# Differential attention: who splits the q, k and v weights, when a finished head is turned, and where the modulation is computed

## The chip, the core and the metric

The kernel runs on one core of a Trainium2 chip. The metric is the device time of one execution in microseconds.

## The reference

`reference` is a stack of two models at 256 tokens and 1024 features, in fp32. The first one has four blocks. Each block has a mixer (0 and 3 Fourier, 1 differential attention, 2 MLA) and a squared-ReLU MLP with 4096 hidden features. Its two inputs, the latent tokens (256) and the context tokens (256), are modulated by 6 vectors of a block, which come from a condition: one condition for the latent tokens, one for the context. The second model (two blocks with a state space mixer and window attention) is not touched by the change.

```
for i in range(DEPTH):
    sh_a, sc_a, g_a, sh_m, sc_m, g_m = split(silu(c) @ mod_w[i] + mod_b[i], 6)     # the same with c_ctx for the context
    h = rms_norm(x, norm_mix_g[i]) * (1 + sc_a) + sh_a
    x = x + g_a * mixer(h_lat, h_ctx)
    h = rms_norm(x, norm_mlp_g[i]) * (1 + sc_m) + sh_m
    x = x + g_m * (square(relu(h @ mlp_w1[i])) @ mlp_w2[i])
# differential attention, 8 heads with two maps of 64 features and a value of 128 each
p = softmax(q1 @ k1.T * scale) - lam * softmax(q2 @ k2.T * scale)      # latent queries: 512 keys, context queries: 256
y = concat(rms_norm(p @ v, subln_g) * (1 - lam_init)) @ w_o
```

Only the latent tokens leave the first model, and block 3's Fourier mixer does not read the context. So of block 2's modulation the context needs shift and scale ahead of the mixer alone (8 of 24 chunks), and of block 3's nothing.

## The kernel before

**Weights.** Every fp32 weight is used as the sum of a high and a low part, with three matmuls in the fast fp32 form (`mm3`, lines 424 to 426) for one product. Weights come in chunks of 1 MB (1024 rows by 256 columns, one `dense` chunk), in the order of `chunks`. SP loads them into raw buffers. `act_split` (L371) copies a chunk to its high part `wh`; `dve_split` (L387) and `pool_split` (L399) subtract to get the low part `wl`, VectorE the first 5/8 of the 2048 columns, GpSimd the rest (`share`, `cut`). There are three slots of `wh`/`wl`. Each engine's instructions are written out in program order, and a split for chunk c is done for c + 2 when the engine comes to chunk c: its slot is that of c - 1, so ScalarE waits until TensorE has used c - 1.

**Raw buffers.** `homes` gives each chunk its raw buffer and `sp_load` loads in the order `self.order`, waiting for the buffer's last user. As long as modulation chunks are still to come, dense chunks alternate between buffers 0 and 1, and modulation chunks use buffer 2 and, every second one in the MLPs, a fourth buffer (`extra`), which lies over other small tiles. Where no modulation chunk is to come, dense chunks take the oldest of three buffers.

**Modulation.** It is computed in two ways. A `mod` chunk is a chunk of `mod_w`: `pe_mod` (L468) multiplies it by the conditions with eight fp32 matmuls of 32 columns by 256 (two passes each), ScalarE copies a pair's rows (`act_mod`, L505), `pe_turn` (L482) turns them with four transposes, and `dve_add` (L523, L525) sums them and adds the bias. A `dmod` chunk is a chunk of the transposed `mod_w`: `pe_condition` (L490) spreads a condition over a PSUM bank pair, and `dve_dmod` (L541 for the context's condition, L546 for the latent one) multiplies and sums in one instruction, two halves of 1024 for a chunk and condition. Block 2's first 16 chunks are `mod` chunks inside the differential attention, one behind each of the twelve q, k and v chunks and four in its tail; its last 8 and the 24 of block 3 are `dmod` chunks in the second MLP, for the latent condition alone.

**Differential attention.** Twelve dense chunks q0 k0 v0 ... q3 k3 v3 (two heads each) and four of w_o. TensorE does a chunk in four parts ("half" 0 to 3). Between the parts lie the attention's steps, `pe_diff_step(s)`, two for three parts, by `beat`: steps 0 to 26 fall into the chunks, 27 to 36 follow one another in the tail, with six or more of the k-blocks of `pe_wo` between them. Unit s is a quarter (128 queries) of head s // 4. In step s TensorE turns the probabilities of unit s - 2 (L1301), computes the scores of s (L1310) and the values of s - 3 (L1321); VectorE takes the maxima (L1469, L1471), ScalarE the exponentials (L1383) and the copy of the turned probabilities (L1392), VectorE joins the two maps (L1489 to L1494). The turn of s waits for the copy of the turn before, which stands behind ScalarE's exponentials of the step, which wait for the maxima. A head's sum is scaled and squared on ScalarE in step 4h + 6 (L1403, L1407), its root is taken on VectorE in step 4h + 7 (L1503 to L1516), and in step 4h + 8 it is turned (`dx`, L1329), copied high (L1413) and low (L1479). The rotary part of q and k (`dve_rope`: L1152, the cosine product L1153, L1156) stands ahead of a step's maxima. Rope, `dx` and the modulation's turns share bank 6.

Where a norm's root is awaited, TensorE is kept at work by fillers (`pe_busy`, L628) or by the condition groups.

Of the kernel before, what the change touches and what calls it, by code (L numbers as in the profile page):

```python
# [111 lines left out]
def chunks(a):  # L112
# [18 lines left out]
    for L in range(4):  # L131
# [5 lines left out]
        elif L == 1:  # L137
            for j in range(4):
                for i, p in enumerate("qkv"):
                    w(("qkv", p, j), a["diff_w_qkv"][0], 0, 8, 1024 * i + 256 * j, 256)  # L140
                    mods(2, 3 * j + i, 3 * j + i + 1)
            mods(2, 12, 16)
# [11 lines left out]
        for n in range(32):  # L154
# [46 lines left out]
class K:  # L201
    def __init__(self, nc, a, out, known):
# [12 lines left out]
        late = [c for c in extra if c > self.ix["mod", 2, 0]]  # L215
        self.extra_first = {extra[0]: (0, 9), late[0]: (2, 7)}
        self.junked = None
        self.dmod_last = [max(c for c, p in enumerate(self.P) if p[0][0] == "dmod" and (p[0][1] < 2) == first) for first in (True, False)]
        self.extra_last = extra[len(extra) - len(late) - 1], late[-1]
# [79 lines left out]
    def homes(self):  # L299
# [78 lines left out]
    def dve_split(self, c, ahead=SLOTS):  # L378
        nc, at, up, DVE = self.nc, self.T.at, self.T.up, self.DVE
        while self.n_dve < self.split_upto(c, ahead):  # L380
# [112 lines left out]
    def act_mod(self, c):  # L493
# [9 lines left out]
        if L == 2 and h < 2:  # L503
            ACT.wait_ge(*at("used", self.extra_last[0]))
# [22 lines left out]
    def dve_dmod(self, c, m):  # L527
# [3 lines left out]
        st = "mlp0" if L < 2 else "mlp1"  # L531
# [3 lines left out]
        if L < 2:  # L535
# [2474 lines left out]
```

## Time and profile before

| | |
|---|---|
| median of 3 runs (lowest, highest) | 3154.44 us (3153.7, 3158.66) |
| the profiled execution's own time | 3153.51 us |
| its span | 3152.2 us |
| mean granted TensorE clock | 0.991 |
| PE, DVE, ACT, POOL busy | 96%, 57%, 47%, 36% of the span |
| first MLP | 165 to 525.3 us |
| differential attention | 525.3 to 831.5 us |
| second MLP | 831.5 to 1189.5 us |
| MLA | 1189.5 to 1340 us |
| third MLP | 1340 to 1531 us |

Times are microseconds from the span's start, unless marked ns. PE is TensorE, PEld its weight load, DVE VectorE, ACT ScalarE, POOL GpSimd, SPq the queue that issues the loads. A row of the timeline has the start, the length, engine, line, operation, what it writes and reads, how many, and in brackets how long its engine was idle before it and what released it. A matmul's length reaches over the start of the next one; the distance of two starts is what one costs.

### The profile page before, as it was taken

To read this page: it belongs to the slowest core of one execution; us is meant where nothing else is said; L and a number is where in the kernel's file an instruction comes from. 1 tells how busy PE (TensorE), PEld (TensorE's weight loads), DVE (VectorE), ACT (ScalarE), POOL (GpSimd) and SP (SyncE) were. 2 spreads that over 40 slices of the span, in tenths; PEclk is the share of its full clock that TensorE was granted. 3 is DMA by queue.
4 is the path that set the end of the run, shared out by engine and by line. 5 is a ranking of instruction groups with operands and counts; after the bars stand their busy time and mean duration, and the time that the engine had idled before them with its cause. 6 is when DMAs were issued, how large, how long until landed. Compare 5 with 4: busy or idle time off the path is not lost.

```text
span 3152.2 us, 49948 instructions
## 1 busy us (share of the span) xinstructions
PE 3025.6 (96%) x20560; PEld 2620.6 (83%) x20560; DVE 1783.2 (57%) x3141; ACT 1486.6 (47%) x2511; POOL 1132.0 (36%) x440
## 2 busy tenths in 40 slices
PE   5999999999999998999999999999999999999999
PEld 3878887776788886699899977878999978779999
DVE  3367775565656446665565555664465466654554
ACT  3453333344443324655465446654355356554553
POOL 0223223110332232245355432444545423434554
PEclk8999999999999999999999999999999999999999
DMA  9345552432456542155345432434555433334554
GB/s 294 121 161 191 196 197 90 142 102 86 139 196 242 200 140 74 52 168 182 112 154 187 143 118 79 119 101 128 169 164 172 149 103 108 97 114 162 159 187 139
DMA packets 423217, 459.92 MB, mean 146 GB/s; under 512 B 9040, under 2 KB 406224, under 8 KB 422992
## 3 DMA queue, kind: packets, MB, share of 16 engines
q1 hardware_dynamic: 419680, 453.32, 44.6%
q8 instruction: 164, 2.69, 0.4%
q10 hardware_dynamic: 3312, 3.42, 0.3%
q14 instruction: 61, 0.50, 0.0%
HBM read 455.66 MB, written 1.05 MB: 145 GB/s over the span
## 4 chain that ended last, share of the span: by engine, by line
PE 83%; DVE 10%; ACT 5%; issue 1%; DMA 1%; ACTq 0%; POOL 0%; DVEq 0%
PE bank L424 23%; PE bank L426 22%; PE bank L425 22%; ACT wh L371 2%; DVE wl L387 1%; PE banks L424 1%; PE banks L425 1%; PE banks L426 1%; PE banks L468 1%; PE bank L628 1%; DVE tmp L730 1%; DVE bc L2488 1%; PE banks L2451 1%; PE bank L1310 1%; DVE xl L738 1%
## 5 line engine op out<-in xcount | busy, mean ns | idle before, releaser
L399 POOL TENSOR_TENSOR wl<-raw,wh 128x768 fp32r<-128x768 f32 (+2 forms) x336 | 1013.9, 3018 | 1845.2 <-ACT wh L371 1835.2
L371 ACT ACTIVATE wh<-raw 128x2048 fp32r<-128x2048 f32 (+1 forms) x336 | 635.9, 1893 | 456.6 <-PE bank L426 423.2
L387 DVE TENSOR_TENSOR wl<-raw,wh 128x1280 fp32r<-128x1280 f32 (+2 forms) x336 | 486.6, 1448 | 524.2 <-ACT wh L371 515.4
L424 PE MATMUL bank<-nh,wh 128*128 128x272 f32 (+1 forms) x1712 | 506.8, 296 | 3.4 <-DVE nl L2036 2.8
L426 PE MATMUL bank<-nh,wl 128*128 128x272 f32 (+1 forms) x1712 | 494.2, 289 | 0.0
L425 PE MATMUL bank<-nl,wh 128*128 128x272 f32 (+1 forms) x1712 | 492.7, 288 | 0.0
L424 PE MATMUL bank<-xh,wh 128*128 128x512 f32 (+2 forms) x1282 | 441.4, 344 | 5.1 <-DVE xl L738 3.7
L426 PE MATMUL bank<-xh,wl 128*128 128x512 f32 (+2 forms) x1282 | 433.8, 338 | 0.0
L425 PE MATMUL bank<-xl,wh 128*128 128x512 f32 (+2 forms) x1282 | 433.7, 338 | 0.0
L424 PE MATMUL bank<-hh,wh 128*128 128x512 f32 (+1 forms) x1024 | 344.1, 336 | 0.0
L425 PE MATMUL bank<-hl,wh 128*128 128x512 f32 (+1 forms) x1024 | 344.1, 336 | 0.0
L426 PE MATMUL bank<-hh,wl 128*128 128x512 f32 (+1 forms) x1024 | 344.1, 336 | 0.0
L424 PEld LDWEIGHTS bank<-nh,wh 128*128 128x128 f32 x1712 | 326.7, 191 | 19.6 <-issue 17.7
L425 PEld LDWEIGHTS bank<-nl,wh 128*128 128x128 f32 x1712 | 326.6, 191 | 0.4
L426 PEld LDWEIGHTS bank<-nh,wl 128*128 128x128 f32 x1712 | 326.3, 191 | 0.0
L424 PEld LDWEIGHTS bank<-xh,wh 128*128 128x128 f32 (+1 forms) x1282 | 242.4, 189 | 46.2 <-issue 10.5
L426 PEld LDWEIGHTS bank<-xh,wl 128*128 128x128 f32 (+1 forms) x1282 | 242.4, 189 | 27.2
L425 PEld LDWEIGHTS bank<-xl,wh 128*128 128x128 f32 (+1 forms) x1282 | 242.6, 189 | 25.0
L424 PEld LDWEIGHTS bank<-hh,wh 128*128 128x128 f32 x1024 | 194.4, 190 | 20.0
L425 PEld LDWEIGHTS bank<-hl,wh 128*128 128x128 f32 x1024 | 194.4, 190 | 19.9
L426 PEld LDWEIGHTS bank<-hh,wl 128*128 128x128 f32 x1024 | 194.4, 190 | 19.9
L839 DVE TENSOR_TENSOR hl<-tmp,hh 128x512 fp32r<-128x512 f32 (+1 forms) x128 | 123.4, 968 | 116.5 <-ACT hh L820 116.5
(452 smaller groups left out, 5544.5 us busy)
## 6 DMA issues: line engine op xcount, KB each, us to landing
raw<-in_mlp_w SPq DMA_DIRECT2D x128, 1024.0 KB, 5.4
raw<-in_w_in SPq DMA_DIRECT2D x60, 1024.0 KB, 5.2
raw<-in_w_mlp_up SPq DMA_DIRECT2D x32, 1024.0 KB, 5.4
raw<-in_w_mlp_down SPq DMA_DIRECT2D x32, 1024.0 KB, 5.1
raw<-in_mod_wT SPq DMA_DIRECT2D x30, 1024.0 KB, 5.4
extra<-in_mod_wT SPq DMA_DIRECT2D x30, 1024.0 KB, 5.6
raw<-in_mod_w SPq DMA_DIRECT2D x23, 1024.0 KB, 5.2
raw<-in_w_in SPq DMA_DIRECT2D x34, 512.0 KB, 4.5
```

Of the source, the lines that this page charges most:

```text
L371: nc.scalar.activation(self.wtile(self.wh, c1), self.rawtile(c1), AF.Copy).then_inc(*up("act_wh", ("wh", c1)))
L387: nc.vector.tensor_tensor(l, r, h.bitcast(F32), ALU.subtract).then_inc(*up("dve_wl", ("wl_dve", c1)))
L399: nc.gpsimd.tensor_tensor(l, r, h.bitcast(F32), ALU.subtract).then_inc(*up("pool_wl", ("wl_pool", c1)))
L424: nc.tensor.matmul(o, ah, bh, start=first, stop=False)
L425: nc.tensor.matmul(o, ah, bl, start=False, stop=False)
L426: return nc.tensor.matmul(o, al, bh, start=False, stop=last)
L468: ins = nc.tensor.matmul(b[q:q + 32, 256 * (i % 2):256 * (i % 2) + 256], self.cst[:, k, :], w[:, k, :], start=(k < 4), stop=(k >= 4))
L628: nc.tensor.matmul(self.bank[bank][:, 0:256], self.ident[:], self.cols[:, 0:256], start=True, stop=True)
L730: nc.vector.scalar_tensor_tensor(out=self.tmp[k % 4][:, cs], in0=self.X[:, k, cs], scalar=A[:, k, s:s + 1], in1=self.spread_root(name)[:, cs],
L738: nc.vector.scalar_tensor_tensor(out=self.xl[:, k, cs], in0=self.tmp[k % 4][:, cs], scalar=self.modv[:, L, 8 * sh + k, s:s + 1], in1=self. ...
L839: nc.vector.tensor_tensor(L[i // 8 % 2][:, i % 8, T], self.ring(st)[i % 4][:, T], H[i // 8 % 2].bitcast(F32)[:, i % 8, T], ALU.subtract).t ...
L1310: nc.tensor.matmul(b[:, 0:ks.stop - ks.start], self.dtile("q", h)[rows, 128 * q:128 * q + 128], self.dtile("k", h)[rows, ks], start=True, ...
```

## The change

It has three parts. **Split.** The chunks of q, k and v get `share` 8: VectorE makes the whole low part, GpSimd none. In all of them but the first, `dve_split` moves from the head of the chunk to the place behind part 1's step, so behind its maxima. **Turns.** `finished` gives the step in which a head is turned and copied: 4h + 9 for heads 0 to 4, 4h + 8 as before for 5 to 7. In the tail `pe_wo(4, 0, 7)` stands in step 35 and `pe_wo(5, 0, 7)` behind step 36. **Modulation.** Block 2's 16 `mod` chunks and all their turns, copies and sums leave the attention. They become `dmod` chunks in the second MLP, the first eight for both conditions, which needs the bank pair 6 and 7 and two more condition groups there. The second MLP then has 36 `dmod` chunks (two behind each dense chunk 8 to 11 and 16 to 19, one behind the others up to 27); the last 12 of block 3 go to the third MLP, one behind every second dense chunk up to 22, all in raw buffer 2, with their own condition groups (`mlp2`) in place of fillers. Dense chunks alternate between buffers 0 and 1 inside the three stretches with modulation chunks only; in the attention they now have three buffers. Cut parts of the diff are the same removals on ScalarE, the same shift of `finished`, and the bookkeeping of the extra buffer and of the last user of the condition banks.

```diff
@@ -137,9 +137,7 @@
                 for i, p in enumerate("qkv"):
-                    w(("qkv", p, j), a["diff_w_qkv"][0], 0, 8, 1024 * i + 256 * j, 256)
-                    mods(2, 3 * j + i, 3 * j + i + 1)
-            mods(2, 12, 16)
+                    w(("qkv", p, j), a["diff_w_qkv"][0], 0, 8, 1024 * i + 256 * j, 256, 8)
@@ -161,12 +159,12 @@
                 dmods(1, n - 4, n - 3)
-            elif L == 1 and n < 8:
-                dmods(2, 16 + n, 17 + n)
-            elif L == 1 and n < 12:
-                dmods(3, 2 * n - 16, 2 * n - 14)
             elif L == 1 and n < 28:
-                dmods(3, n - 4, n - 3)
+                i = n + max(0, min(n, 12) - 8) + max(0, min(n, 20) - 16)
+                for i in range(i, i + (2 if n // 4 in (2, 4) else 1)):
+                    dmods(2 + i // 24, i % 24, i % 24 + 1)
+            elif L == 2 and n < 24 and n % 2 == 0:
+                dmods(3, 12 + n // 2, 13 + n // 2)
@@ -305,14 +303,16 @@
         dmods = [c for c in mods if self.P[c][0][0] == "dmod"]
+        stage = lambda c: 0 if c not in dmods else int(self.dmod_stage(c)[-1])
+        spans = [([c for c in mods if stage(c) == i][0], [c for c in mods if stage(c) == i][-1]) for i in range(3)]
...
                 d = self.nth[c]
-                t = d % 2 if self.dense[max(d - 4, 0)] < mods[-1] else min(range(RAWS), key=lambda i: last[i])
+                t = d % 2 if any(lo < c and self.dense[max(d - 4, 0)] < hi for lo, hi in spans) else min(range(RAWS), key=lambda i: last[i])
...
                 t = m % EARLY if m < 2 * EARLY else (2, 5, 6, 7)[m - 2 * EARLY] if m < 20 else 2
-                if c in dmods and dmods.index(c) % 2:
+                if c in dmods and stage(c) < 2 and dmods.index(c) % 2:
@@ -321,10 +321,19 @@
-            while late and d > 3 and (late[0] < self.dense[d - 3] or c == self.ix["wo", 2] and late[0] < self.ix["mod", 2, 14]):
+            while late and d > 3 and late[0] < self.dense[d - 3]:
...
+    def dmod_stage(self, c):
+        _, L, i = self.P[c][0]
+        return "mlp0" if L < 2 else "mlp1" if L == 2 or i < 12 else "mlp2"
+    def dmod_conditions(self, c):
+        _, L, i = self.P[c][0]
+        return 2 if L < 2 or L == 2 and i < 8 else 1
@@ -384,7 +393,7 @@
             r, h, l = self.rawtile(c1)[:, 0:n], self.wtile(self.wh, c1)[:, 0:n], self.wtile(self.wl, c1)[:, 0:n]
-            nc.vector.tensor_tensor(l, r, h.bitcast(F32), ALU.subtract).then_inc(*up("dve_wl", ("wl_dve", c1)))
+            nc.vector.tensor_tensor(l, r, h.bitcast(F32), ALU.subtract).then_inc(*up("dve_wl", ("wl_dve", c1), *([("wl_pool", c1)] if n == self.P[c1][2] * self.P[c1][3] else [])))
@@ -392,6 +401,9 @@
             n = self.cut(c1)
+            if n == self.P[c1][2] * self.P[c1][3]:
+                self.n_pool += 1
+                continue
@@ -528,11 +538,11 @@
         _, L, i = self.P[c][0]
-        st = "mlp0" if L < 2 else "mlp1"
+        st, S = self.dmod_stage(c), self.dmod_conditions(c)
...
         DVE.wait_ge(*at("raw", c))
-        if L < 2:
+        if S == 2:
@@ -599,12 +609,13 @@
     def pe_root(self, name, T):
-        if name in ("mlp0", "mlp1"):
+        if name in ("mlp0", "mlp1", "mlp2"):
...
             self.pe_condition(name, 0, 1)
-            if name == "mlp0":
+            if name == "mlp2":
+                self.pe_busy(1)
+            else:
                 self.pe_condition(name, 1, 0)
-            self.pe_busy(1 if name == "mlp1" else 0)
@@ -1182,6 +1193,13 @@
+    def finished(self, s):
+        for h in range(8):
+            if s == (9 if h < 5 else 8) + 4 * h:
+                return h
+        return None
@@ -1219,8 +1237,6 @@
                             roping = None
-                        if st == 1:
-                            self.pe_turn()
@@ -1247,27 +1263,17 @@
                             roping = None
-                        if half == 1:
-                            self.pe_turn()
...
                             roping = w, 2 * j + m
-                self.pe_mod(c + 1, (7,), (6,))
...
             self.pe_diff_step(s)
-            if s == 28:
-                self.pe_turn()
-            if s in (27, 29, 34):
-                self.pe_mod(self.ix["mod", 2, 12 + (27, 29, 34).index(s)], (7,) if s < 30 else (3,), (6,))
-            if s == 31:
-                self.pe_turn()
-            if 29 <= s < 33 or s == 35:
-                self.pe_wo(min(s - 29, 4), 0, 6)
+            if 29 <= s < 33:
+                self.pe_wo(s - 29, 0, 6)
+            elif s >= 35:
+                self.pe_wo(s - 31, 0, 7)
         for g in range(8):
-            self.pe_wo(g, 6 if g < 5 else 0, 8)
-            self.pe_turn()
-            if g == 1:
-                self.pe_mod(self.ix["mod", 2, 15], (3,), (6,))
+            self.pe_wo(g, 6 if g < 4 else 7 if g < 6 else 0, 8)
@@ -1350,11 +1356,8 @@
                     self.act_diff_step(self.beat(w, j, half))
-                self.act_mod(c + 1)
...
             self.act_diff_step(s)
-            if s == 29:
-                self.act_mod(self.ix["mod", 2, 13])
@@ -1429,28 +1430,19 @@
                             roping = None
+                        self.dve_diff_step(self.beat(w, j, half))
                         if half == 1:
-                            self.dve_add()
-                        self.dve_diff_step(self.beat(w, j, half))
+                            self.dve_split(c)
...
                             roping = w, 2 * j + half // 2
-                self.dve_mod(c + 1)
...
             self.dve_diff_step(s)
-            if s == 28:
-                self.dve_add()
-            if s == 29:
-                self.dve_mod(self.ix["mod", 2, 13])
             if s == 31:
-                self.dve_add()
...
                 self.dve_resid(("wo", 2 * j + m), 1, 2, 2 * j + m, BOTH, "mlp1")
-                self.dve_add()
-            if j == 0:
-                self.dve_mod(self.ix["mod", 2, 15])
@@ -1472,8 +1464,8 @@
             self.dve_diff_root(h)
-        h, b = divmod(s - 8, 4)
-        if b == 0 and 0 <= h < 8:
+        h = self.finished(s)
+        if h is not None:
```

## Rows read from the trace of the kernel before

**Rows 1.** The page: busy time of each engine; a DMA issue's KB and landing.
```profile
PE 3025.6 (96%) x20560; PEld 2620.6 (83%) x20560; DVE 1783.2 (57%) x3141; ACT 1486.6 (47%) x2511; POOL 1132.0 (36%) x440
...
raw<-in_mlp_w SPq DMA_DIRECT2D x128, 1024.0 KB, 5.4
```

**Rows 2.** Windows: attention, second MLP, third MLP; busy us of each engine.
```profile
525.30:831.50 306.20, 288.73 (x1782) 219.69 (x1781) 182.10 (x473) 130.15 (x288) 48.62 (x22) 0.99 0.33 108
...
831.50:1189.50 358.00, 356.10 (x1596) 292.60 (x1595) 190.64 (x297) 130.19 (x152) 105.95 (x38) 1.00 0.54 189
...
1340.00:1545.00 205.00, 200.97 (x1650) 196.60 (x1648) 119.13 (x145) 108.86 (x153) 108.71 (x41) 0.99 0.54 174
```

**Rows 3.** Timeline of TensorE, steps 26 to 29: start, length, idle before it.
```profile
754.31 0.65 PE L1301 MATMUL banks<-ident,de 128*128 128x128 f32 x4
...
758.18 0.66 PE L1301 MATMUL banks<-ident,de 128*128 128x128 f32 x4 [0.95 <-ACT dpt L1392]
...
762.50 1.07 PE L468 MATMUL banks<-raw,cst 128*32 128x256 f32 x16 [1.95 <-DMA raw<-in_mod_w]
...
763.50 0.44 PE L1301 MATMUL banks<-ident,de 128*128 128x128 f32 x2
...
769.70 0.66 PE L482 MATMUL banks<-ident,mrow 128*128 128x128 f32 x4 [3.17 <-DVE dol L1479]
...
772.96 1.88 PE L468 MATMUL banks<-raw,cst 128*32 128x256 f32 x16
...
774.77 0.50 PE L424 MATMUL bank<-doh,wh 128*128 128x512 f32 x1
```

**Rows 4.** Windows, two microseconds of the same stretch; the granted clock ahead of DMA.
```profile
772.00:774.00 2.00, 2.00 (x16) 1.32 (x20) 1.37 (x3) 0.57 (x1) 0.00 (x0) 0.50 0.00 0
```

**Rows 5.** Lines, 525.3 to 831.5: busy us, mean ns, idle before and releaser.
```profile
L1301 PE MATMUL banks<-ident,de 128*128 128x128 f32 x96 | 16.1, 276 | 4.9 <-ACT dpt L1392 4.9
...
L482 PE MATMUL banks<-ident,mrow 128*128 128x128 f32 x32 | 4.9, 276 | 5.0 <-DVE dol L1479 5.0
...
L1329 PE MATMUL banks<-ident,rs 128*128 128x128 f32 x8 | 1.3, 286 | 1.2 <-DVE tmp L1152 1.2
```

**Rows 6.** Timeline of all engines in a k chunk.
```profile
597.77 1.49 DVE L387 TENSOR_TENSOR wl<-raw,wh 128x1280 fp32r<-128x1280 f32 x1 [3.02 <-ACT wh L371]
...
597.81 3.12 POOL L399 TENSOR_TENSOR wl<-raw,wh 128x768 fp32r<-128x768 f32 x1 [13.09 <-ACT wh L371]
...
599.51 1.70 DVE L1153 TENSOR_TENSOR dq<-dq,rt 128x256 f32<-128x256 f32 x1
...
604.96 0.66 PE L1301 MATMUL banks<-ident,de 128*128 128x128 f32 x4 [1.18 <-ACT dpt L1392]
```

**Rows 7.** One source line: the cosine product of k, ns min/median/max.
```profile
L1153 DVE TENSOR_TENSOR dk<-dk,rt x8: 410/415/1720, 557.6 to 743.1; 128x256 f32<-128x256 f32 x8
```

**Rows 8.** Timeline of all engines: wo 3's high part and GpSimd's low part.
```profile
811.00 1.91 ACT L371 ACTIVATE wh<-raw 128x2048 fp32r<-128x2048 f32 x1
...
815.54 1.86 POOL L399 TENSOR_TENSOR wl<-raw,wh 128x768 fp32r<-128x768 f32 x1
```

**Rows 9.** Lines, second MLP: one kind of modulation reduction.
```profile
L546 DVE CUSTOM_DVE_ANT_0 extra<-extra,banks,cols 128x1024 f32<-128x1024 f32 x32 | 40.8, 1275 | 5.2 <-DMA extra<-in_mod_wT 5.2
```

**Rows 10.** Timeline of TensorE, first MLP: a condition group in the open.
```profile
197.91 1.05 PE L490 MATMUL banks<-ident,cst 128*128 128x128 f32 x8
```

**Rows 11.** Timeline of all engines in the third MLP.
```profile
1353.17 3.15 POOL L399 TENSOR_TENSOR wl<-raw,wh 128x768 fp32r<-128x768 f32 x1 [12.15 <-ACT wh L371]
...
1359.94 1.90 ACT L371 ACTIVATE wh<-raw 128x2048 fp32r<-128x2048 f32 x1
...
1365.70 1.90 ACT L371 ACTIVATE wh<-raw 128x2048 fp32r<-128x2048 f32 x1
```

**Rows 12.** DMA issues, 935 to 975: KB each, us to landing.
```profile
extra<-in_mod_wT SPq DMA_DIRECT2D x4, 1024.0 KB, 7.4
...
raw<-in_mlp_w SPq DMA_DIRECT2D x4, 1024.0 KB, 9.8
```

More of the change, by code:

```diff
@@ L214, in __init__ @@
         extra = [c for c in sorted(self.home) if self.home[c] == EXTRA]
-        late = [c for c in extra if c > self.ix["mod", 2, 0]]
-        self.extra_first = {extra[0]: (0, 9), late[0]: (2, 7)}
+        self.extra_first = {extra[0]: (0, 9)}
         self.junked = None
-        self.dmod_last = [max(c for c, p in enumerate(self.P) if p[0][0] == "dmod" and (p[0][1] < 2) == first) for first in (True, False)]
-        self.extra_last = extra[len(extra) - len(late) - 1], late[-1]
+        self.dmod_last = [max(c for c, p in enumerate(self.P) if p[0][0] == "dmod" and self.dmod_stage(c) == st) for st in ("mlp0", "mlp1", "mlp2")]
+        self.dmod_both = max(c for c, p in enumerate(self.P) if p[0][0] == "dmod" and self.dmod_conditions(c) == 2)
+        self.extra_last = extra[-1]
         self.loaded = self.n_act = self.n_dve = self.n_pool = 0
@@ L502, in act_mod @@
             ACT.wait_ge(*at("acc", "modT", *self.pairs[n - 2]))
-        if L == 2 and h < 2:
-            ACT.wait_ge(*at("used", self.extra_last[0]))
         nc.scalar.activation(self.mrow[n % 2][:], self.place["mod", L, h][:], AF.Copy).then_inc(*up("act_row", ("row", L, h), ("out", "mod", L, h)))
@@ L542, in dve_dmod @@
                                            accum_out=self.modv[:, L, 2 * i + m, 1:2]
-                                           ).then_inc(*up("dve_dmod", ("dsum", L, 1, i, m), *([("out", "cb", st, 1, 0), ("out", "cb", st, 1, 1)] if final else [])))
+                                           ).then_inc(*up("dve_dmod", ("dsum", L, 1, i, m), *([("out", "cb", st, 1, 0), ("out", "cb", st, 1, 1)] if m and (final or c == self.dmod_both) else [])))
         DVE.wait_ge(*at("cb", st, 0, 0))
@@ L774, in pe_mlp @@
                         self.pe_group(c, m, slot, X, T, (st, "h", i + m), m == 1)
-                if i == 2 and st == "mlp0":
+                if i == 2 and st in ("mlp0", "mlp1"):
                     self.pe_condition(st, 1, 1)
@@ L1366, in act_diff @@
                 square = 2 * j + m
-            if j == 0:
-                self.act_mod(self.ix["mod", 2, 15])
         self.act_square("mlp1", 7, self.X[:, 7, :], BOTH)
@@ L1407, in act_diff_step @@
             nc.scalar.activation(self.tmp[2][:], o[:], AF.Square).then_inc(*up("act_do", ("dsq", h)))
-        h, b = divmod(s - 8, 4)
-        if b == 0 and 0 <= h < 8:
+        h = self.finished(s)
+        if h is not None:
             ACT.wait_ge(*at("acc", "dx", h))
@@ L1422, in dve_diff @@
                 c = self.ix["qkv", w, j]
-                self.dve_split(c)
                 if w == "q" and j == 0:
+                    self.dve_split(c)
                     self.dve_diff_rope("q", 0)
@@ L1431, in dve_diff @@
                             roping = None
+                        self.dve_diff_step(self.beat(w, j, half))
                         if half == 1:
-                            self.dve_add()
-                        self.dve_diff_step(self.beat(w, j, half))
+                            self.dve_split(c)
                         if w != "v" and half % 2:
                             roping = w, 2 * j + half // 2
-                self.dve_mod(c + 1)
         for s in range(self.LAST_BEAT + 1, 37):
             self.dve_diff_step(s)
-            if s == 28:
-                self.dve_add()
-            if s == 29:
-                self.dve_mod(self.ix["mod", 2, 13])
             if s == 31:
-                self.dve_add()
                 self.dve_split(self.ix["wo", 0])
@@ L1450, in dve_diff @@
                 self.dve_resid(("wo", 2 * j + m), 1, 2, 2 * j + m, BOTH, "mlp1")
-                self.dve_add()
-            if j == 0:
-                self.dve_mod(self.ix["mod", 2, 15])
     def dve_diff_rope(self, w, h):
@@ L1474, in dve_diff_step @@
             self.dve_diff_root(h)
-        h, b = divmod(s - 8, 4)
-        if b == 0 and 0 <= h < 8:
+        h = self.finished(s)
+        if h is not None:
             H, L = self.dout(h)
@@ L1746, in act_latent_high @@
         keys, T, g, dim, parts = self.latent(u)
-        ACT.wait_ge(*at("used", self.extra_last[1]))
+        ACT.wait_ge(*at("used", self.extra_last))
         for n, (H, L) in enumerate(parts):
```

## The prediction

> **What bounds the kernel now.** I read the page first: TensorE is busy for 96% of the span, VectorE for little more than half of it [rows 1]. The reader is to see that there is little to gain by making another engine quicker; time goes away only where TensorE has less to do, or stops waiting. Then I read the stretches one by one [rows 2]. The differential attention (525.3 to 831.5 us) keeps TensorE busy for 288.7 of 306.2 us, the MLP behind it for 356.1 of 358.0. So TensorE's work in the attention is paid in full, some 17 us of waiting are there to be won, and the MLP has next to none. I then went through the attention in order of time, engine beside engine, to see which instruction each TensorE wait hangs on. Last I read the loads' landing times, because the change moves 16 MB of them.
>
> **The sixteen modulation chunks leave the attention.** Each is eight fp32 matmuls, sixteen passes. The next instruction starts 1.00 us after the first of them (762.50 to 763.50 [rows 3]). Fifteen at 1.0 us and one at 1.8 us (772.96 to 774.77, with a granted clock of 0.50 [rows 3, 4]) are 16.8 us. The eight turns of their rows are listed at 4.9 us in all, 0.6 each [rows 5]; the next instruction overlaps their ends, as with the chunk, so I count 0.5 each, 4 us. This is certain work of the bounding engine. I share it out by place: eleven chunks and five turns in the body (steps up to 26), 11.0 + 2.5, the rest behind it.
>
> **Waits in the body.** In a k chunk VectorE's cosine product takes 1.70 us, because it begins while GpSimd's part of a weight split runs (597.81 to 600.93 [rows 6]); undisturbed it takes 0.415 us [rows 7]. The maxima stand behind it, and TensorE waits 1.18 us at 604.96 [rows 6]. Three such places make most of the 4.9 us that the turns of the probabilities (L1301) wait; 0.95 of it is step 27, so 3.9 lie in the body [rows 3, 5]. With q, k and v split by VectorE alone, and only behind the maxima, nothing of GpSimd is in the way and the 1.3 us come back: these waits go. The modulation turns waited 5.0 us for bank 6, 3.17 of them at 769.70 [rows 3, 5]; 1.8 go in the body. The turn of a finished head waited 1.2 us in the group shown [rows 5], since the normalisation a step before was just late; one step later this goes too. Together 6.9 us. The copies of the modulation's rows on ScalarE, its sums on VectorE and the third raw buffer for the attention's weights I count at nothing: no TensorE wait of the body hangs on them.
>
> **What VectorE pays for it.** The split of 2048 columns does not stand in the trace. Its lower bound is today's 1.49 us for 1280 columns; by proportion it is 2.4; the upper bound is 1.49 plus GpSimd's 3.12 for the rest, 4.6 [rows 6]. I take 2.3 to 2.4, being the same instruction with more columns. In k and v chunks it falls into a gap between steps. In q chunks it falls between two steps that follow each other. Where a head's root is in the same step (q of the third and fourth group) I carry it forward: the maxima come 2.3 us late, ScalarE copies the next q late, and TensorE waits some 0.35 us for it, twice: 0.7. At 4.6 us it would be 2.3 us more each time. Body: 11.0 + 2.5 + 6.9 - 0.7 = 19.7 us.
>
> **The tail of the attention.** From 754.31 to 774.77 TensorE runs steps 26 to 29 with three chunks and one turn as filling [rows 3]. The filling goes, but the chain stays: a step's turns may start only when ScalarE has copied the turn before, 3.9 us after the last step (754.31 to 758.18). Head 4's low half now stands in step 25 ahead of the probabilities, some 1.2 us. So I set 5.1 for step 26, 3.9 for 27, 6.3 for 28 (the root of head 5 stands before its probabilities), 2.2 for 29's own work, and keep 1.3 for the slow clock: 18.8 against 20.5 us, a gain of 1.7, bounds 0 and 4. Afterwards two chunks, two turns and 0.6 us of waits go, 3.6 us. Against it stands a new wait. The matmuls of wo groups 4 and 5 are now issued before the last head is done, so after group 1 only 18 matmuls separate the release of wo 0's slot from the first use of wo 3, which lands in that slot. At 358.0/1536 = 0.233 us each [rows 2] this is 4.2 us. The high part starts at 811.00 and GpSimd's low part ends at 817.40, behind a square [rows 8]: 6.4 us, and 0.3 us from release to start without the modulation's row copy. 6.7 - 4.2 = 2.5 us. The tail gives 1.7 + 3.6 - 2.5 = 2.8 us, and the attention 22.5 in all.
>
> **The second MLP.** It gets 36 transposed chunks instead of 32, eight of them for both conditions: 88 reductions instead of 64, 24 at 1.3 us [rows 9] = 31 us on VectorE. The cover is its idle time: 190.6 of 358.0 us busy [rows 2]. Were it gone, a chunk's low part would be late by at most 2.6 us, which the three slots cover. TensorE pays for two condition groups of four matmuls: one takes 1.05 us in the open [rows 10]; the other stands in the root's latency instead of a filler, 0.2. Cost 1.25.
>
> **The third MLP.** It gets 12 chunks, 24 reductions on VectorE (31 us; busy 119 of 205 [rows 2]), and its two conditions take the place of fillers: nothing. But they take raw buffer 2, so a weight load waits for the buffer of two chunks before, not three. Chunks come every 5.76 us (1359.94 to 1365.70 [rows 11]). The loop of a buffer is a landing of 5.4 [rows 1], 1.9 for the high part and 3.15 for the low one: 10.6 with the semaphores, against 11.5 allowed. With another load beside it the landing is longer; the rows of a stretch with three loads to a chunk have 7.4 and 9.8 [rows 12], the low bound is 5.4. At first, chunk 4 can be loaded only at 1356.3 [rows 11], lands at 1361.8 and is 1.9 us late for ScalarE; behind it there are some 3 us before TensorE needs it. I count 0.3 us; bounds 0 and 10 (below). The loads that leave the attention only empty its queue: SP waits for nothing there that TensorE needs, but for the 1.95 us at 762.50, already counted.
>
> **Sum.** -22.5 + 1.25 + 0.3 = -20.9, say 21 us. The profiled execution took 3153.5 us (span 3152.2), the median is 3154.4, so 3132.5 and **3133.4 us**.
>
> **Rivals.** (a) The forecast, 62%: 3133, own range 3126 to 3141. (b) VectorE becomes the bound of the steps, 15%. Its split grows by some 0.9 us in twelve chunks; if each one delays a step in full, 11 us of the gain go: 3144. For it: the steps wait for the maxima already. Against it: GpSimd's interference of 1.3 us goes at the same places, and nine of twelve splits fall in gaps. A rule speaks for (b): the Trainium skill, Perfetto Trace Analysis, "Optimizing Scalar/DVE Operations", advises to offload from VectorE when it is saturated, and warns that GpSimd shares its port; by its first half the sum is that of (b), by the warning that of (a). The trace shows the warning's case, 1.70 against 0.415. (c) The tail goes to the lower clock, 11%. Today one stretch stands at 0.50, i.e. 1.2 GHz, after TensorE was little busy, and the chunk there took 1.8 instead of 1.0 us [rows 3, 4]. With the filling gone TensorE idles ahead of three steps; if all of them and wo's first 18 matmuls (4.2) ran at half speed, that is 4.2 plus some 1.3 for each step, 8 us: 3141. [...] (d) Slower, 5%: the two raw buffers of the third MLP. Weight loads of which three run together landed in 9.8 us [rows 12]; the loop is then 15.0 against 11.5, 3.5 us for every second chunk, over 12 pairs 42 less the slack of 3: 39, and the kernel ends at 3172. It decides from a landing of 8.3 on ((21 + 3)/12 = 2.0 a pair); at 7.4 it costs 10 us (12.6 against 11.5, twelve times, less 3). Against it: only two loads meet here. (e) The gain is given back in parts and nothing remains within the measurement, 3%: 3154. (f) Larger than the range, 4%: the wait for wo 3 does not come and the tail's steps run closer: 3124.
>
> **The numbers.** The range goes from 3126 to 3145 and holds (a), (b) and (c) nearly in full, 82%. Below it lies (f), above it (d), (e) and the worst of (b). 0.2% (6.3 us) is about what a measurement of this kernel can tell from no change. Faster by more: (a), (b), (c), (f), 91%; within: 4%; slower: 5%.
>
> **What would show it.** No L468 or L482 behind the first MLP; the attention near 284 us, with TensorE waits of under 10; the cosine product at 0.42 us throughout; a split of 2.3 us in q, k, v; a wait of some 2.5 us before wo group 6; the granted clock in steps 27 to 29; the second MLP 1.2 us longer; in the third no wait of TensorE for a low part. I am wrong if the splits delay the maxima in k and v chunks too, if the tail's steps cost more than their chain, or if the third MLP's loads land over 7 us after issue.

## The result, and the profile after

The changed kernel takes 3129.9 us (median of four runs, 3126.8 to 3131.6) against 3154.4: a ratio of 0.9918, 95% interval 0.9901 to 0.9936. The forecast was 3133.4. The profiled execution has a span of 3127.9 us, 24.3 less than before; 21 were forecast. The kernel is faster by far more than 0.2%, but the parts of the gain don't lie where the prediction put them.

The page, part 1, of the changed kernel:

```profile
PE 3006.5 (96%) x20294; PEld 2616.1 (84%) x20294; DVE 1824.5 (58%) x3221; ACT 1482.2 (47%) x2503; POOL 1102.0 (35%) x428
```

The windows of its attention, second and third MLP (length, busy time of PE, PEld, DVE, ACT and POOL, clock, DMA share, GB/s):

```profile
524.42:802.85 278.43, 264.99 (x1491) 209.78 (x1491) 175.28 (x457) 125.35 (x280) 21.48 (x12) 0.99 0.17 54
802.85:1161.78 358.93, 357.37 (x1610) 294.27 (x1609) 218.20 (x345) 130.21 (x152) 104.90 (x38) 1.00 0.58 200
1314.48:1505.83 191.35, 190.54 (x1596) 189.33 (x1595) 127.29 (x170) 103.82 (x145) 104.46 (x39) 1.00 0.76 252
```

Beside [rows 2]: the attention is 27.7 us shorter (forecast 22.5), the second MLP 0.9 longer (forecast 1.25), the third takes 191.35 us as before (1340.95 to 1532.30 there; forecast 0.3 more). The stage ahead of the attention is 0.9 shorter, the MLA between the MLPs 1.25 and the rest behind 2.2 longer; the change has no instruction in the last two. 20 us of the MLA stand at a clock of 0.91 where the kernel before had 1.00, and behind the third MLP the stretches of 20 us below full clock lack 1.12 of a stretch in sum (22 us) against 0.96 (19 us) before. So these 3.5 us go with the clock. Two runs below bear this out for the MLA: `split_only` and `turns_only` leave the modulation as it was before, and in their profiled executions the MLA takes 152.30 and 152.71 us, like the changed kernel's 152.70 and unlike the 151.45 of the kernel before. In sum it is 24.3.

TensorE's waits in the attention fall from 17.5 to 13.4 us (length less busy time); the prediction had set under 10 as a sign, which did not come.

The attention's waits, in the groups of its lines (busy, mean ns | idle before, released by):

```profile
L1307 PE MATMUL banks<-ident,de 128*128 128x128 f32 x96 | 15.9, 274 | 7.1 <-ACT dpt L1393 7.1
L436 PE MATMUL bank<-doh,wh 128*128 128x512 f32 x30 | 12.6, 419 | 2.5 <-issue 2.5
L1157 PE MATMUL banks<-dq,perm 128*128 128x256 f32 x16 | 5.0, 394 | 1.0 <-ACT dq L1357 1.0
```

L1307 is the turn of the probabilities (L1301 before). All its 7.1 us lie in the tail: in the body nothing waits but the rope of q (1.0). The tail in TensorE's timeline, with the place before wo group 6:

```profile
730.02 0.60 PE L1307 MATMUL banks<-ident,de 128*128 128x128 f32 x4
...
734.51 0.66 PE L1307 MATMUL banks<-ident,de 128*128 128x128 f32 x4 [2.62 <-ACT dpt L1393]
...
738.39 0.44 PE L1307 MATMUL banks<-ident,de 128*128 128x128 f32 x2 [1.50 <-ACT dpt L1393]
...
744.42 0.44 PE L1307 MATMUL banks<-ident,de 128*128 128x128 f32 x2 [3.01 <-ACT dpt L1393]
...
790.15 0.47 PE L436 MATMUL bank<-doh,wh 128*128 128x512 f32 x1 [2.48 <-issue]
...
791.60 0.63 PE L438 MATMUL bank<-doh,wl 128*128 128x512 f32 x1
792.03 0.63 PE L436 MATMUL bank<-doh,wh 128*128 128x512 f32 x1
```

Steps 26 to 28 cost 4.49, 3.88 and 6.03 us, and the wait before wo group 6 is the forecast 2.5. Behind it matmuls start every 0.43 instead of 0.23 us, a granted clock of about half, 1.2 GHz; eight of them make 1.6 us:

```profile
791.00:794.00 3.00, 3.00 (x9) 2.35 (x8) 3.00 (x5) 0.53 (x1) 2.86 (x3) 0.52 0.00 0
```

The cosine product of k is no longer slow anywhere (min/median/max ns; L1153 before [rows 7]):

```profile
L1164 DVE TENSOR_TENSOR dk<-dk,rt x8: 412/416/416, 555.5 to 719.5; 128x256 f32<-128x256 f32 x8
```

### The profile page after: what moved, and what is told of

It reads as the page before. It is cut to its first block, busy times and chain, and to the rows that moved or that the text cites. A ratio compares the mean times of both kernels' runs of the same rounds, so it can differ in the third digit from the quotient of the medians.

```text
span 3127.9 us, 49466 instructions
## 1 busy us (share of the span) xinstructions
PE 3006.5 (96%) x20294; PEld 2616.1 (84%) x20294; DVE 1824.5 (58%) x3221; ACT 1482.2 (47%) x2503; POOL 1102.0 (35%) x428
## 4 chain that ended last, share of the span: by engine, by line
PE 85%; DVE 9%; ACT 4%; issue 1%; DMA 0%; ACTq 0%; POOL 0%; DVEq 0%
PE bank L436 23%; PE bank L438 23%; PE bank L437 23%; ACT wh L380 2%; DVE wl L396 1%; PE banks L436 1%; PE banks L437 1%; PE banks L438 1%; PE bank L1316 1%; PE bank L639 1%; DVE tmp L741 1%; DVE bc L2480 1%; PE banks L1327 1%; PE banks L2443 1%; PE banks L1157 1%
## 5 line engine op out<-in xcount | busy, mean ns | idle before, releaser
L411 POOL TENSOR_TENSOR wl<-raw,wh 128x768 fp32r<-128x768 f32 (+2 forms) x324 | 981.9, 3031 | 1849.3 <-ACT wh L380 1839.3
L396 DVE TENSOR_TENSOR wl<-raw,wh 128x1280 fp32r<-128x1280 f32 (+3 forms) x336 | 495.0, 1473 | 502.7 <-ACT wh L380 493.9
L763 DVE SCALAR_TENSOR_TENSOR X<-bank,modv,X 128x256 f32<-128x256 f32 x210 | 94.6, 479 | 132.4 <-PE bank L438 132.2
```

The source lines that it names most:

```text
L411: nc.gpsimd.tensor_tensor(l, r, h.bitcast(F32), ALU.subtract).then_inc(*up("pool_wl", ("wl_pool", c1)))
L763: nc.vector.scalar_tensor_tensor(out=self.X[:, k, cs], in0=o[:, cs], scalar=self.modv[:, L, 8 * gate + k, s:s + 1], in1=self.X[:, k, cs], ...
```

## The experiments

Each is compared over one stretch, the **body**: from the attention's first weight matmul to the start of step 26, in the profiled execution. The expectations for `mods`, `share5`, `head8`, `turns` and `split_only` count it from the attention's start, 8.3 us earlier (229.0 us for the kernel before, 205.6 for the changed one): take 8.3 off their figures to compare them with what follows. Here it is for the kernel before and the changed one (533.61 and 532.71 are those first matmuls), 220.70 and 197.31 us:

```profile
533.61:754.31 220.70, 212.78 (x1332) 163.59 (x1333) 137.05 (x348) 97.53 (x219) 31.11 (x12) 1.00 0.31 101
```

```profile
532.71:730.02 197.31, 196.29 (x1137) 156.63 (x1137) 129.77 (x334) 94.34 (x214) 3.75 (x2) 1.00 0.20 63
```

**Modulation alone** (`mods`). The changed kernel with the split and the turns as before.

```diff
-                    w(("qkv", p, j), a["diff_w_qkv"][0], 0, 8, 1024 * i + 256 * j, 256, 8)
+                    w(("qkv", p, j), a["diff_w_qkv"][0], 0, 8, 1024 * i + 256 * j, 256)
                 c = self.ix["qkv", w, j]
+                self.dve_split(c)
...
-                        if half == 1:
-                            self.dve_split(c)
...
-            if s == (9 if h < 5 else 8) + 4 * h:
+            if s == 8 + 4 * h:
```

> Only the modulation is moved; the splits (share 5, at the head of the chunk) and the turns (4h + 8) are as in the kernel before. Theory of the prediction: the body takes 229.0 - 11.0 (chunks) - 2.5 (their turns) - 1.8 (their waits for bank 6) = 213.7 us, and the cosine product beside GpSimd still costs its 1.7 us, with 3 to 4 us of waits for the copied probabilities. The rest of the kernel is as in the changed one, so the whole takes 3129.9 + 8.1 = 3138. Rival: the modulation's matmuls were cover for waits that VectorE and GpSimd cause; with them gone these grow by what was covered, and the body takes 217 us or more (3142 and above), with over 8 us of TensorE waits in it.

Measured: 3149.9 us (ratio 0.9973, 0.9963 to 0.9983), and a body of 218.33 us: the modulation's work is gone and the body is only 2.4 shorter. The rival is right: it set 208.7 or more in this count, the theory 205.4. The window has a clock of 0.96 over its length, and TensorE's groups show where it waits:

```profile
532.90:751.23 218.33, 204.71 (x1136) 161.89 (x1137) 135.72 (x338) 94.29 (x214) 31.15 (x12) 0.96 0.18 58
...
656.00:665.00 9.00, 6.12 (x20) 4.48 (x20) 4.14 (x14) 4.89 (x16) 0.00 (x0) 0.62 0.37 117
...
L1307 PE MATMUL banks<-ident,de 128*128 128x128 f32 x72 | 12.9, 292 | 7.6 <-ACT dpt L1393 7.6
L1335 PE MATMUL banks<-ident,rs 128*128 128x128 f32 x8 | 1.3, 287 | 3.6 <-DVE tmp L1163 3.6
```

With the three smaller L1335 groups (1.8, 0.3, 0.3) the body waits 13.6 us, and three stretches of 24 us in all stand at 0.72, 0.62 and 0.62. The changed kernel's body, with the same matmuls, has 1.0 us of waits and 196.29 us of busy time where this one has 204.71. So the 21.0 us between the two are 12.6 of waits and 8.4 of slower matmuls. One of the waits, read engine beside engine:

```profile
651.71 1.49 DVE L396 TENSOR_TENSOR wl<-raw,wh 128x1280 fp32r<-128x1280 f32 x1 [0.37 <-ACT wh L380]
653.12 0.42 DVE L1163 TENSOR_TENSOR tmp<-banks,rt 128x256 f32<-128x256 f32 x1
653.45 1.74 DVE L1164 TENSOR_TENSOR dq<-dq,rt 128x256 f32<-128x256 f32 x1
655.29 0.42 DVE L1167 TENSOR_TENSOR dq<-dq,tmp 128x256 f32<-128x256 f32 x1
655.64 1.28 DVE L1459 TENSOR_REDUCE sm<-bank 128x1 f32<-128x512 f32 x2
...
651.75 3.15 POOL L411 TENSOR_TENSOR wl<-raw,wh 128x768 fp32r<-128x768 f32 x1 [11.73 <-ACT wh L380]
...
658.93 1.11 PE L1307 MATMUL banks<-ident,de 128*128 128x128 f32 x4 [2.88 <-ACT dpt L1393]
```

VectorE waits for the high part with the rope and the maxima queued behind; its split then pushes the cosine product into GpSimd's 3.15 us. In the kernel before, the modulation's chunk and its turn stood in this time.

**Fillers where the modulation stood** (`modsfill`). Run mods, and

```diff
+                if (j, w) != (3, "v"):
+                    self.pe_busy(3, 7)
```

> The kernel in which only the modulation is moved (run mods), with six filler matmuls (1.26 us) behind eleven of the twelve q, k and v chunks, where the modulation chunks stood: 13.9 us of TensorE work that computes nothing, as much as the eleven chunks and five turns of the body had. Theory A (the modulation's matmuls were cover for waits, and kept the clock up): from the attention's first weight matmul to step 26 the run without them took 218.3 us, the kernel before 220.7; the fillers take the place of waits (13.6 us) and of the lower clock (some 8 us), and the stretch takes 217 to 222 us. Theory B (the waits came from what moved with the modulation: bank 6, the buffers, the loads): the fillers come on top, 232 us.

Measured: 3147.3 us (0.9969, 0.9956 to 0.9982) and a body of 215.22 us, with 13.9 us more work for TensorE than in mods. Theory A holds, and the body is shorter than its 217 to 222 us. The fillers are a stand-in and not an equal: they add some 15 us to TensorE's busy time (211.40 against 196.29 us in the changed kernel, both at full clock), the modulation had added 16.5. In the profiled executions the stretch is 3.1 us shorter with the useless work than without it (the medians don't tell the two kernels apart). Its waits are 2.3 us for the copy and 1.5 for the heads' turns:

```profile
532.25:747.47 215.22, 211.40 (x1202) 169.22 (x1203) 132.51 (x338) 94.75 (x214) 31.11 (x12) 1.00 0.19 59
...
L1309 PE MATMUL banks<-ident,de 128*128 128x128 f32 x72 | 12.0, 276 | 2.3 <-ACT dpt L1395 2.3
L1337 PE MATMUL banks<-ident,rs 128*128 128x128 f32 x8 | 1.3, 287 | 1.0 <-DVE tmp L1163 1.0
```

**Who splits** (`share5`) **and where** (`head8`). Of the changed kernel, once the share of 8 is undone, once the place.

```diff
-                    w(("qkv", p, j), a["diff_w_qkv"][0], 0, 8, 1024 * i + 256 * j, 256, 8)
+                    w(("qkv", p, j), a["diff_w_qkv"][0], 0, 8, 1024 * i + 256 * j, 256)
```

> The changed kernel with one thing undone: GpSimd again makes 3/8 of the low part of q, k and v; VectorE's 5/8 stays behind the maxima of part 1. The body of the attention (524.4 us to step 26) took 205.6 us in the changed kernel. Theory of the prediction: what counted was GpSimd beside the cosine product (1.70 instead of 0.415 us), at three places ahead of maxima that TensorE waits for. GpSimd's part starts as soon as the high part is there, so the product is slow again, and the body gets 3 us longer (209), less the two waits of 0.49 us for the copy of q, which the longer split caused: 208. Rival: the place behind the maxima did it, and the longer split on VectorE is a cost: the cosine product stays at 0.42 us wherever TensorE waits for it, the body takes 204.6 to 205.6.

```diff
                 c = self.ix["qkv", w, j]
+                self.dve_split(c)
...
-                        if half == 1:
-                            self.dve_split(c)
```

> The changed kernel with one thing undone: VectorE still makes the whole low part of q, k and v, but at the head of the chunk, ahead of the maxima, as before. Theory of the prediction: the place matters, since a split of 2.3 us ahead of the maxima holds them up where VectorE waits for the high part first: 0.3 to 1 us in a chunk, the body (205.6 us in the changed kernel) gets 3 to 8 us longer, with TensorE waiting for the copied probabilities. Rival: VectorE has time at the head of a chunk (it is busy for half of the span), the body takes 205.6 to 206.6.

Measured: share5 3129.9 us (0.9918, 0.9901 to 0.9934), a body of 197.31, the changed kernel's to the hundredth. head8 3140.4 us (0.9948, 0.9933 to 0.9963), a body of 206.65. Beside the other two parts the place is worth 9.3 us (3 to 8 were expected), and behind the maxima it makes no difference who splits:

```profile
532.10:729.41 197.31, 196.35 (x1137) 156.52 (x1138) 129.75 (x334) 94.00 (x214) 22.19 (x12) 1.00 0.20 63
...
L1307 PE MATMUL banks<-ident,de 128*128 128x128 f32 x72 | 11.8, 273 | 0.5 <-ACT dpt L1393 0.5
L1157 PE MATMUL banks<-dq,perm 128*128 128x256 f32 x16 | 5.0, 394 | 0.4 <-ACT dq L1357 0.4
```

```profile
533.67:740.32 206.65, 200.34 (x1137) 158.88 (x1138) 131.15 (x334) 93.99 (x214) 4.93 (x2) 0.98 0.19 62
...
L1307 PE MATMUL banks<-ident,de 128*128 128x128 f32 x72 | 12.0, 276 | 3.5 <-ACT dpt L1393 3.3
L1335 PE MATMUL banks<-ident,rtt 128*128 128x128 f32 x4 | 0.7, 287 | 1.8 <-DVE tmp L1163 1.8
```

GpSimd is busy 22.19 us in share5's body and TensorE waits no longer than without it (0.9 against 1.0). Its twelve parts take 1.80 to 1.95 us there, since with VectorE's part behind the maxima the two seldom run side by side; in mods seven of the twelve took 3.11 to 3.15 us. Of sixteen cosine products three are slow (1.72, 1.07 and 0.92 us), all in the first two chunk groups. head8 has GpSimd only for two chunks of wo's weights and waits 6.3 us all the same, 3.5 for the copy and 2.8 for turns, plus a lower clock in two places (0.72 over 6 us each, 3.4 us). One of these waits, 1.92 us with a lower clock behind it, does follow a cosine product of 1.71 us beside GpSimd's part of wo 0; the others have no GpSimd near. With the split at the head of the chunk the share was not changed alone, so what it is worth there is not shown. The body of mods is 21.0 us longer than the changed kernel's, the place and the turns undone one at a time make it 9.3 and 6.2 longer, and the 5.5 us left over may hold it.

**Turns undone** (`turns`). `if s == 8 + 4 * h` in `finished`, else the changed kernel.

> The changed kernel with one thing undone: heads 0 to 4 are turned in step 4h + 8 again. Theory of the prediction: the turn then waits for the normalisation, 1.2 us in all, and the copies stand in a step that is busier: body 205.6 + 1.2 = 206.8 us, the wait on the row of the turn (L1335) in the list of groups. Rival: without GpSimd's splits VectorE's normalisation is in time by itself, and the later turn gives nothing: 205.6, no wait on that row.

Measured: 3138.4 us (0.9941, 0.9926 to 0.9956), a body of 203.54: 6.2 us more, five times the theory. TensorE waits 3.0 us for turns and 1.5 for the copy of step 22, and behind the latter the clock is low (0.72 over 6 us, 1.7 us):

```profile
L1307 PE MATMUL banks<-ident,de 128*128 128x128 f32 x72 | 12.0, 276 | 1.5 <-ACT dpt L1393 1.5
L1335 PE MATMUL banks<-ident,sq 128*128 128x128 f32 x4 | 0.7, 287 | 1.3 <-DVE tmp L1163 1.3
```

The releaser is not the normalisation (L1508 here) but L1163, the rope's first product. It frees bank 6, which the turn needs, and it stands in VectorE's queue behind the root and the weight split. [rows 5] names the same releaser (L1152) for its 1.2 us. The place of the first of two waits of 1.35 us, and then what stands before the wait in step 22:

```profile
635.54 0.69 DVE L1508 TENSOR_TENSOR rtt<-rtt,sm 128x512 f32<-128x512 f32 x1
637.06 2.28 DVE L396 TENSOR_TENSOR wl<-raw,wh 128x2048 fp32r<-128x2048 f32 x1
639.26 0.42 DVE L1163 TENSOR_TENSOR tmp<-banks,rt 128x256 f32<-128x256 f32 x1
639.74 0.66 PE L1335 MATMUL banks<-ident,rtt 128*128 128x128 f32 x4 [1.35 <-DVE tmp L1163]
...
700.99 1.81 POOL L411 TENSOR_TENSOR wl<-raw,wh 128x768 fp32r<-128x768 f32 x1 [179.64 <-ACT wh L380]
701.02 2.06 DVE L1164 TENSOR_TENSOR dq<-dq,rt 128x256 f32<-128x256 f32 x1
```

The normalisation is done 3.5 us before the turn; the split of 2.28 us, which the change itself put there, holds up the rope. And the wait for the copy follows no turn: GpSimd's part of wo 0 meets the cosine product, which takes 2.06 us and holds up the maxima of step 22. In the changed kernel the product starts 0.7 us before GpSimd's part (698.95 and 699.63) and takes 0.41. So of the 6.2 us only the 3.0 of waits for turns belong to the turns for certain; some 3.2 come from a meeting that a shift of time brought about.

**One part each on the kernel before** (`split_only`, `turns_only`), by the same edits made there.

> The kernel before with the split part alone: VectorE makes the whole low part of q, k and v, in all chunks but the first behind part 1's step; modulation chunks stay in the attention, heads are turned in step 4h + 8. From the four runs so far: the place of the split was worth 10 us where the modulation was gone, since waits of 1.4 to 1.9 us and the lower clock behind them came back without it. Theory A (the modulation's matmuls cover the same waits, so the parts only pay together): here the split can win back only what TensorE waits for the copied probabilities in the body, 3.9 us; the body (229.0 us in the kernel before) takes 225, the whole some 3150. Theory B (each part is worth what it was worth beside the others, 10 us): body 219, the whole 3144.

> The kernel before with the turns alone: heads 0 to 4 are turned and copied in step 4h + 9. From the first weight matmul to step 26 the kernel before took 220.7 us, with 2.05 us of waits of the turn of a head for its normalisation. Next to the moved splits and without the modulation the later turn was worth 6.2 us. Theory A (parts pay together, each alone wins only the waits that stand in this kernel): 2 us or less, 218.7. Theory B (the turn has a worth of its own): 214.5.

Measured: split_only 3151.7 us (0.9981, 0.9972 to 0.9990), body 215.50, 5.2 less; turns_only 3154.2 us (0.9994, 0.9985 to 1.0003), body 219.24, 1.5 less. Theory A is the nearer one in both: in this count it set 216.7 and 218.7, theory B 210.7 and 214.5. In split_only the wait for the copy is nearly gone (3.9 before), that of the turns has grown from 2.05 to 2.8:

```profile
L1304 PE MATMUL banks<-ident,de 128*128 128x128 f32 x72 | 12.0, 275 | 0.3 <-ACT dpt L1395 0.3
L1332 PE MATMUL banks<-ident,sq 128*128 128x128 f32 x4 | 0.7, 286 | 1.4 <-DVE tmp L1155 1.4
```

The grown waits are two of 1.35 us, the same as in turns and at the same place, though the modulation is still there: they come from the longer split ahead of the rope. So the parts pay together for two reasons. The modulation covered waits, and the moved split makes a wait that the later turn takes away. The parts alone give 5.2 + 1.5 + 2.4 = 9.1 us of body, together 23.4.

**The tail.** `late5` moves four k-blocks of wo group 5 behind group 4; `busy` puts fillers before group 6; `early` moves 18 k-blocks into the waits of steps 27 to 32.

```diff
-                self.pe_wo(s - 31, 0, 7)
+                self.pe_wo(s - 31, 0, 7 if s == 35 else 3)
...
-            self.pe_wo(g, 6 if g < 4 else 7 if g < 6 else 0, 8)
+            self.pe_wo(g, (6, 6, 6, 6, 7, 3, 0, 0)[g], 8)
```

> The changed kernel with one thing moved: of wo group 5 only three k-blocks stand behind step 36, the other four are done with its last, behind groups 0 to 4. Same instructions. Between the release of wo 0's slot and the first use of wo 3 lie 30 matmuls (7.0 us) instead of 18 (4.2 us). If the wait of 2.48 us before group 6 is the slot's loop (high part, then GpSimd's low part behind a square, 6.7 us), it goes, and with it the lower clock behind it (8 matmuls at 0.43 instead of 0.23 us, 1.6 us): from step 36 to the end of the attention 4.1 us less, 3125.8. If the wait hangs on something else (the load of wo 3, a bank), it stays at 2.5 us.

```diff
+            if g == 6:
+                self.pe_busy(11)
```

> The changed kernel with eleven filler matmuls of 256 columns (about 2.3 us in all) in the wait before wo group 6. They do nothing for the result. If the lower clock behind that wait (8 matmuls at 0.43 instead of 0.23 us) comes from the wait, it goes and the time between group 6's first matmul and the attention's end is 1.6 us shorter, with the first matmul where it was; the whole 3128.3. If it comes from the little work of the steps before, it stays.

```diff
+            for g, k0, k1 in {27: ((0, 0, 4),), 28: ((0, 4, 5), (1, 0, 1)), 29: ((1, 1, 5),), 30: ((2, 0, 3),), 31: ((0, 5, 6), (1, 5, 6), (2, 3, 4)), 32: ((2, 4, 6),)}.get(s, ()):
+                self.pe_wo(g, k0, k1)
             self.pe_diff_step(s)
-            if 29 <= s < 33:
-                self.pe_wo(s - 29, 0, 6)
+            if s == 32:
+                self.pe_wo(3, 0, 6)
```

> The changed kernel with 18 k-blocks of wo groups 0 to 2 moved from behind steps 29 to 31 into the waits of steps 27 to 32: 4, 2, 4, 3, 3, 2 of them. Same instructions. In the changed kernel step 26 starts at 730.0 and step 32 at 762.6, 32.6 us. If the steps are bound by their chain (scores, maxima, exponentials, copy: 4.5, 3.9, 6.0, 5.6, 3.8, 3.8 us), the same stretch takes 27.6 us and the kernel 5 us less, 3125. If the waits of 2.6, 1.5 and 3.0 us had been hidden work of the later steps anyway, nothing changes.

Measured: late5 3123.6 us (0.9893, 0.9874 to 0.9913). From step 32 to the next MLP's first weight matmul it takes 44.28 against 48.52 us, 4.2 less as expected; the wait and the lower clock are gone. busy 3132.0 us (0.9919, 0.9898 to 0.9940): a filler is two matmuls, so the eleven took 4.6 us and group 6 starts at 791.85, later than without them. But what follows shows the point: from group 6 to the next MLP 19.47 us against 20.97, 1.5 less. So the lower clock came from the 2.5 us wait and cost 1.5. early 3123.0 us (0.9890, 0.9873 to 0.9907): steps 26 to 32 take 27.84 us against 32.58, where 27.6 was worked out from the chain:

```profile
729.75 0.60 PE L1309 MATMUL banks<-ident,de 128*128 128x128 f32 x4
...
744.14 0.44 PE L1309 MATMUL banks<-ident,de 128*128 128x128 f32 x2 [0.25 <-ACT dpt L1395]
749.84 0.66 PE L1309 MATMUL banks<-ident,de 128*128 128x128 f32 x4 [1.50 <-ACT dpt L1395]
...
757.59 0.44 PE L1309 MATMUL banks<-ident,de 128*128 128x128 f32 x2
```

From step 32 to the next MLP early takes 49.46 us, 0.9 more than the changed kernel, so that 3.8 of the 4.7 us are left of it in the attention. The profiled attention of late5 is only 1.4 us shorter than the changed kernel's, as its steps 26 to 32 had a low clock (last section).

**Together** (`both`, and `both5` with share 5): early's blocks, two k-blocks of group 5 ahead of the turn of head 7, two behind it, four behind group 4.

> The changed kernel with the tail of the attention rearranged, same instructions: 18 k-blocks of wo groups 0 to 2 in the waits of steps 27 to 32 (as in run early), two k-blocks of group 5 ahead of the turn of head 7 and four behind group 4 (more than in run late5 stand between the release of wo 0's slot and wo 3). By the two runs with one part each: 4.7 us less to step 32, less 0.9 behind it, 2.5 of wait and 1.6 of lower clock less, and 0.8 of wait ahead of the turn of head 7: 8.7 us less than the changed kernel, 3121. If the parts share a wait, 3124.

> As run both, with GpSimd making 3/8 of the low part of q, k and v again (share 5). Next to the unchanged tail the two shares took the same time from the first weight matmul to step 26 (197.31 and 197.31 us), so the same is expected here, within 0.3 us of profiled time in that stretch. If VectorE's longer split held up the steps anywhere, this one is faster there.

Measured: both 3121.1 us (0.9885, 0.9870 to 0.9900), both5 3121.1 (0.9885, 0.9868 to 0.9901). Attention from first weight matmul to the next MLP's: 270.0 and 269.9 us against 278.4. The wait before group 6 is 0.49 us; expected were none and 8.7 us, it is 8.4. Both beat the changed kernel; the bodies are 197.38 and 197.31, so that the share again makes no difference.

## Why the prediction was right, and where its steps were not

**The total** is near, 24.3 against 21 us, in part by luck: the attention gave 5.2 us more than forecast, and 3.5 us were lost to the clock behind it. The body gave 23.4 instead of 19.7, steps 26 to 29 4.2 instead of 1.7, and the attention behind them 0.2 instead of 1.1.

**The modulation's work** is gone, and it was more than counted: in the body TensorE's busy time falls by 16.5 us (212.78 to 196.29), not 13.5. From first start to next start the chunks and turns do take the 13.5. Most of the rest lies at the seams, where their neighbours take longer. In the kernel before, four matmuls of the values take 0.47 us ahead of a weight matmul and 0.64 ahead of a modulation chunk, and the weight matmul behind the chunk takes 0.33 instead of 0.23:

```profile
692.15 0.71 PE L1321 MATMUL banks<-dv,dpt 128*128 128x128 f32 x4
692.62 0.36 PE L424 MATMUL bank<-wh,xh 128*128 128x256 f32 x1
...
696.77 0.71 PE L1321 MATMUL banks<-dv,dpt 128*128 128x128 f32 x4
697.41 1.07 PE L468 MATMUL banks<-raw,cst 128*32 128x256 f32 x16
698.42 0.50 PE L424 MATMUL bank<-xh,wh 128*128 128x512 f32 x1
698.75 0.40 PE L425 MATMUL bank<-xl,wh 128*128 128x512 f32 x1
```

As a term of its own this step failed: the prediction called it "certain work of the bounding engine". Alone it gives 2.4 us of body, since the same matmuls covered waits and kept the clock up; with fillers in their place the body is 3.1 us shorter than with nothing there (modsfill). It paid because the two other parts stood beside it.

**Waits in the body.** Forecast 6.9 less 0.7, measured 7.9 less 1.0. The two 0.49 us waits for the copy of q are the forecast 0.35 twice. But the reason given, "nothing of GpSimd is in the way", is wrong in its first half: share5 keeps GpSimd and has the same body. The place behind the maxima does it (9.3 us beside the other parts): at the head of the chunk VectorE waits for the high part with the rope and the maxima queued behind, three times for 1.3 to 2.0 us in head8. GpSimd beside the cosine product is a cost of its own: where wo 0's part meets it, in turns and head8, waits of 1.5 and 1.9 us follow. The split of 2048 columns takes 2.28 us, as taken.

**The turns.** Their wait was put down to the normalisation being late. It is bank 6, held until VectorE comes to the rope, and the moved split of 2.28 us made that later: 2.05 us of such waits in the body before (the prediction read the 1.2 of one group), 2.8 with the split part alone, 3.0 in turns. The 6.2 us of turns, where 1.2 were forecast, are these 3.0 and some 3.2 that go with step 22.

**The tail.** Steps 26 to 29 win 4.2 us, not 1.7: I kept 1.3 us for a slow clock that didn't come there, and the steps were shorter by 0.6, 0, 0.3 and 0.3 than set. The wait of 2.5 us before group 6 came in place and size. What was missing is the lower clock behind it, 1.5 us: rival (c) named the mechanism, for another place.

**The rivals.** (b), VectorE bound: it is busy 129.8 of 197.3 us in the body, and undoing its longer split gives nothing. (d): in the third MLP the weights land in a median of 5.6 us and the modulation in 7.2, under the 8.3 from which it decides, and the stage has not moved. That the MLA and the rest would take 3.5 us more, at a lower clock, was in no part of the prediction; why the clock falls there in one execution and not in another isn't known.

## What to carry to other kernels

Work that runs in the gaps of a latency chain is not worth its busy time. Before it is taken out, ask which waits it covers and lay them open: here 16.5 us of matmuls were worth 2.4 alone, and three edits of 9 us in sum were worth 23 together. An instruction that waits for something late goes behind those that somebody waits for; then look what stands behind it in turn, here the rope and with it a bank. Behind the maxima it made no difference which engine did the split. And where a chain leaves gaps, put the next stage's matmuls into them (early: 4.7 us in those steps with the same instructions, 0.9 of it given back behind them).

## What was not expected of the hardware

The granted clock fell to half behind single waits of 1.5 to 2.9 us (turns, mods, the wait before group 6), but not always: the waits of 2.62, 1.50 and 3.01 us in steps 27 to 29 left it at 1.00 in the changed kernel, while share5 and late5, with the same instructions there, had it low. Waits of 1.78 us in mods (at 618, 679 and 740 us) left it at 1.00 too. From the start of step 26 to that of step 32 (windows):

In share5:

```profile
729.41:762.03 32.62, 28.22 (x141) 20.36 (x140) 20.67 (x73) 15.63 (x44) 0.65 (x1) 0.90 0.03 11
```

In late5:

```profile
731.68:767.00 35.32, 28.19 (x140) 20.23 (x139) 20.74 (x73) 15.65 (x44) 0.63 (x1) 0.90 0.03 9
```

Share5 takes 32.62 us, against 32.58 at full clock, since the slower matmuls fell into the waits for ScalarE. In late5 the low clock reached the blocks of w_o behind, and it cost 2.7 us. Late5's four runs took 3121.1, 3121.2, 3125.9 and 3127.5 us (the profiled one); those of early, which fills most of these waits, lie within 1 us.
